# Routing in groups of 3, 3, 2 and 1 token tiles, with the mixes four tiles ahead

## The reference

```
mix = concatenate([y_ml, y_rg], axis=-1).astype(x.dtype) @ lp['w_out']
x = x + g1 * mix
hn2 = rmsnorm(x, lp['norm2']) * (1 + sc2) + sh2
...
s = jax.nn.sigmoid(x2d.astype(jnp.float32) @ router_w.astype(jnp.float32))
sb = s + router_bias.astype(jnp.float32)
grp = sb.reshape(N, N_GROUPS, N_EXPERTS // N_GROUPS)
gscore = jnp.sum(lax.top_k(grp, 2)[0], axis=-1)
_, gidx = lax.top_k(gscore, TOPK_GROUPS)
...
_, eidx = lax.top_k(jnp.where(emask, sb, -jnp.inf), TOP_K)
wts = wts / jnp.sum(wts, axis=-1, keepdims=True) * ROUTED_SCALE
```

## Time and profile before

| | us |
|---|---|
| median of 3 runs (2456.18 to 2460.27) | 2458.14 |
| the profiled execution | 2452.43 |
| its span, first to last instruction | 2450.7 |
| PE busy | 2045.1 (83%) |
| DVE busy | 1286.7 (53%) |
| ACT busy | 1012.7 (41%) |
| POOL busy | 689.4 (28%) |

### The profile page before, as it was taken

How to read it: one execution, slowest core, us unless ns; L and a number is a source line. 1 busy time by engine, 2 the same in 40 slices (tenths; PEclk the granted TensorE clock), 3 DMA queues, 4 the chain that set the end, 5 groups by cost and what they waited for, 6 DMA issues and landing times. The chain is left out here.

```text
span 2450.7 us, 30697 instructions
## 1 busy us (share of the span) xinstructions
PE 2045.1 (83%) x8155; PEld 1336.8 (55%) x8156; DVE 1286.7 (53%) x2145; ACT 1012.7 (41%) x1458; POOL 689.4 (28%) x648
## 2 busy tenths in 40 slices
PE   2776998999868979817999999999999999999940
PEld 0232433447767835405766666676666666666730
DVE  1547343300456758855555555565555454555547
ACT  0334433200112311105665555666665555556631
POOL 4010010000000012452344444443444444444420
PEclk7898998999879989958999999999999999999975
DMA  9422230110100063109978989867888989996454
GB/s 264 132 81 85 69 104 18 43 35 18 27 1 1 6 252 117 69 28 340 320 205 282 318 249 323 231 172 198 247 278 273 351 268 317 299 301 176 106 149 180
DMA packets 114241, 424.52 MB, mean 173 GB/s; under 512 B 22933, under 2 KB 37269, under 8 KB 89229
## 3 DMA queue, kind: packets, MB, share of 16 engines
q1 hardware_dynamic: 62508, 261.05, 28.8%
q0 software_dynamic: 51376, 162.80, 26.4%
q10 hardware_dynamic: 304, 0.02, 0.0%
HBM read 338.68 MB, written 85.66 MB: 173 GB/s over the span
## 5 line engine op out<-in xcount | busy, mean ns | idle before, releaser
L1726 DVE TENSOR_TENSOR wupl<-w,wuph 128x2048 fp32r<-128x2048 f32 x232 | 521.4, 2289 | 546.4 <-ACT wuph L1692 546.4
L1692 ACT ACTIVATE wuph<-w 128x2048 fp32r x232 | 432.0, 1916 | 37.9 <-SPq L1522 34.0
L1643 PE MATMUL bank<-w,hT 128*128 x912 | 414.1, 597 | 0.7 <-issue 0.3
L1625 PE MATMUL bank<-wuph,xTh 128*128 128x512 f32 x920 | 370.1, 402 | 22.1 <-DVE xTl L1735 22.0
L1625 PE MATMUL bank<-wuph,xTl 128*128 128x512 f32 x920 | 361.9, 393 | 0.0
L1625 PE MATMUL bank<-wupl,xTh 128*128 128x512 f32 x920 | 361.0, 392 | 0.0
L1643 PEld LDWEIGHTS bank<-w,hT 128*128 128x128 f32 x912 | 165.0, 191 | 169.2 <-issue 169.1
L1577 POOL DMA_INDIRECT xg<-hn_scratch,idx_g x118 | 215.4, 1825 | 96.0 <-POOL idx_g L1569 93.9
L1585 POOL DMA_INDIRECT yacc_scratch<-y,idx_s x114 | 185.1, 1623 | 113.8 <-ACT y L1683 67.0
L1682 ACT ACTIVATE y<-bank 128x512 f32<-128x512 f32 x114 | 68.2, 598 | 358.1 <-POOLq L1582 201.9
L1625 PEld LDWEIGHTS bank<-wuph,xTh 128*128 128x128 f32 x920 | 174.6, 190 | 61.3 <-issue 27.5
(11 more groups left out here) (312 smaller groups left out, 2340.9 us busy)
## 6 DMA issues: line engine op xcount, KB each, us to landing
w<-in_exp_w SPq DMA_DIRECT2D x192, 1024.0 KB, 9.0
wada<-in_w_ada POOLq DMA_DIRECT2D x16, 1024.0 KB, 5.9
wg<-in_w_in SPq DMA_DIRECT2D x12, 1024.0 KB, 5.5
x<-x_scratch SPq DMA_DIRECT2D x18, 512.0 KB, 4.0
wada<-in_w_ada SPq DMA_DIRECT2D x4, 2048.0 KB, 21.2
yacc_scratch<-zero POOLq DMA_DIRECT2D x10, 512.0 KB, 9.1
x_scratch<-x SPq DMA_DIRECT2D x9, 512.0 KB, 2.6
hn_scratch<-hn SPq DMA_DIRECT2D x9, 512.0 KB, 2.9
```

The source lines that it names most:

```text
L1625: mm = pe.matmul(b_up[j][:, :], x[:, k, :], w[:, :, k, :], start=(k == 0 and i == 0), stop=(k == KT - 1 and i == 2))
L1643: mm = pe.matmul(b_down[half][:, :], hT[:, i, :], w2[:, bass.ds(slot, 1), i, half * 512:(half + 1) * 512].rearrange("p s n -> p (s n)"), s ...
L1692: act.activation(part13(wup[j][0], half), raw13(e % WSLOT, half), ACT.Copy).then_inc(w_high, 1)
L1726: dve.tensor_tensor(part13(wup[j][1], half), raw13(e % WSLOT, half), part13(wup[j][0], half).bitcast(F32), ALU.subtract).then_inc(w_low, 1)
```

## The change

x and hn get six buffers each (NB = 6), and the mixes three pairs of banks in place of two. The tiles are handled in GROUPS of 3, 3, 2 and 1. For a group DVE takes all residuals, then works out one root for all its columns, then makes its rows one after the other. The first group's residuals, root and rows stand ahead of everything; a later group's residuals lie one by one between the choice and the slots of the tiles of the group before, and its root and rows behind the last of them. ACT squares the tiles of the next group behind the exponential (NEXT) and ahead of the ranks. PE runs mixes 0 to 3 at the start; mix t+4 comes in two halves, one between the transposes and the score of tile t, one between the score and the counts. SP loads six x tiles at the start and stores group by group.

The core of the diff:

```diff
+    NB = 6
+    GROUPS = [(0, 1, 2), (3, 4, 5), (6, 7), (8,)]
+    LEAD = 4
+    NEXT = {t: after[j] for group, after in zip(GROUPS, GROUPS[1:]) for j, t in enumerate(group) if j < len(after)}
...
-            for t in range(1, NT):
+            for t in range(1, NB):
                 load_x(t)
-                store(t - 1)
-            store(NT - 1)
+            for group in GROUPS:
+                for t in group:
+                    store_x(t)
+                for t in group:
+                    store_h(t)
+                    if t + NB < NT:
+                        load_x(t + NB)
...
+            def mix(t, half):
+                if t >= 3 and half == 0:
+                    pe.wait_ge(x2_new, t - 2)
...
-            mix(0)
+            for t in range(LEAD):
+                mix(t, 0)
+                mix(t, 1)
             pe.wait_ge(s_in, m.n_route)
             for t in range(NT):
-                if t + 1 < NT:
-                    mix(t + 1)
                 pe.wait_ge(hn_new, t + 1)
...
+                if t + LEAD < NT:
+                    mix(t + LEAD, 0)
                 bank = ring.fill()
...
                 ring.filled(mm)
+                if t + LEAD < NT:
+                    mix(t + LEAD, 1)
                 if t >= 1:
                     places(t - 1)
...
                 ring.drained(act.activation(ex[t % 2][:, :], bank[:, 0:NE], ACT.Exp, scale=-1.0))
+                if t in NEXT:
+                    square(NEXT[t])
                 if t >= 1:
                     place_out(t - 1)
...
+            def norm(group):
+                dve.wait_ge(x2_sq, group[-1] + 1)
+                c = slice(group[0], group[-1] + 1)
+                v = ss[:, c]
                 link(dve.tensor_scalar(v, v, 1.0 / D, EPS, ALU.mult, ALU.add))
-                newton_rsqrt(link, dve, v, rs[:, :], rt[:, :], ri[:, :])
...
+                newton_rsqrt(link, dve, v, rs[:, c], rt[:, c], ri[:, c])
+                for t in group:
+                    s, h = min(t, 1), hn[t % NB]
+                    link(dve.scalar_tensor_tensor(h[:, :], x[t % NB][:, :], rs[:, t:t + 1], scale[s], ALU.mult, ALU.mult))
+                    dve.tensor_tensor(h[:, :], h[:, :], shift[s], ALU.add).then_inc(hn_new, 1)
...
-            residual(0)
-            for t in range(NT):
-                if t + 1 < NT:
-                    residual(t + 1)
-                pick(t)
-                if t >= 1:
-                    slots(t - 1)
+            for t in GROUPS[0]:
+                add(t)
+            norm(GROUPS[0])
+            for group, after in zip(GROUPS, GROUPS[1:] + [()]):
+                for j, t in enumerate(group):
+                    pick(t)
+                    if j < len(after):
+                        add(after[j])
+                    if t >= 1:
+                        slots(t - 1)
+                    if j + 1 == len(after):
+                        norm(after)
```

More of the change, by code:

```diff
@@ L1138, in stage_route @@
         n2row = sb("n2row", [P, D])
-        x = [sb(f"x2_{j}", [P, D]) for j in range(2)]
-        hn = [sb(f"hn2_{j}", [P, D]) for j in range(2)]
+        x = [sb(f"x2_{j}", [P, D]) for j in range(NB)]
+        hn = [sb(f"hn2_{j}", [P, D]) for j in range(NB)]
         sq = sb("sq4", [P, D])
@@ L1178, in load_x, with store_x, store_h @@
             def load_x(t):
[L1179 to L1185, removed]
+                if t >= NB:
+                    sp.wait_ge(hn_new, t - NB + 1)
+                    sp.wait_ge(s_x2[0], 48)
+                sp.dma_start(x[t % NB][:, :], m.x1[t * P:(t + 1) * P, :]).then_inc(s_x[(t // 3) % 2], 16)
+            def store_x(t):
                 sp.wait_ge(x2_new, t + 1)
-                sp.dma_start(m.x2[rows, :], x[t % 2][:, :]).then_inc(s_x2[t % 2], 16)
+                sp.dma_start(m.x2[t * P:(t + 1) * P, :], x[t % NB][:, :]).then_inc(s_x2[t >= 3], 16)
+            def store_h(t):
                 sp.wait_ge(hn_new, t + 1)
-                sp.dma_start(m.hn2[rows, :], hn[t % 2][:, :]).then_inc(s_hn[t % 2], 16)
+                sp.dma_start(m.hn2[t * P:(t + 1) * P, :], hn[t % NB][:, :]).then_inc(s_hn[t >= 3], 16)
             load_x(0)
@@ L1228, in _ @@
             ring = Ring(pe, m.ring, full, free)
[L1230 to L1238, removed]
+            def mix(t, half):
+                if t >= 3 and half == 0:
+                    pe.wait_ge(x2_new, t - 2)
+                bank = m.banks[2 + 2 * (t % 3) + half]
+                for k in range(KT):
+                    mm = pe.matmul(bank[:, :], m.yT[:, k, t * P:(t + 1) * P], wo[:, k, half * 512:(half + 1) * 512],
+                                   start=(k == 0), stop=(k == KT - 1))
+                if half:
+                    mm.then_inc(mixed, 1)
             def places(t):
@@ L1257, in _ @@
                         kk = 4 * half + k
-                        mm = pe.transpose(bank[:, k * P:(k + 1) * P], hn[t % 2][:, kk * P:(kk + 1) * P], m.ident)
+                        mm = pe.transpose(bank[:, k * P:(k + 1) * P], hn[t % NB][:, kk * P:(kk + 1) * P], m.ident)
                     ring.filled(mm)
+                if t + LEAD < NT:
+                    mix(t + LEAD, 0)
                 bank = ring.fill()
@@ L1287, in place_out, with square @@
                 ring.drained(act.activation(rank[t % 2][:, :], bank[:, 0:NE], ACT.Copy))
-            for t in range(NT):
+            def square(t):
                 act.wait_ge(x2_new, t + 1)
@@ L1292, in _ @@
                     act.wait_ge(x2_sq, t)
-                act.activation(sq[:, :], x[t % 2][:, :], ACT.Square, accum_out=ss[:, t:t + 1]).then_inc(x2_sq, 1)
+                act.activation(sq[:, :], x[t % NB][:, :], ACT.Square, accum_out=ss[:, t:t + 1]).then_inc(x2_sq, 1)
+            for t in GROUPS[0]:
+                square(t)
+            for t in range(NT):
                 for half in range(2):
@@ L1320, in _, with add @@
                 link(dve.scalar_tensor_tensor(scale[s], scale[s], 1.0, n2row[:, :], ALU.add, ALU.mult))
-            def residual(t):
+            def add(t):
                 s = min(t, 1)
                 dve.wait_ge(mixed, t + 1)
[L1325 to L1329, removed]
+                dve.wait_ge(s_x[(t // 3) % 2], 48 * (t // NB + 1))
+                if t >= NB:
+                    dve.wait_ge(s_hn[0], 48)
+                    dve.wait_ge(full, jobs(t - NB) + 2)
+                h = hn[t % NB]
@@ L1330, in residual @@
                 for half in range(2):
                     c = slice(half * 512, (half + 1) * 512)
-                    ins = dve.tensor_tensor(h[:, c], m.banks[2 + 2 * (t % 2) + half][:, :], gate[s][:, c], ALU.mult)
+                    ins = dve.tensor_tensor(h[:, c], m.banks[2 + 2 * (t % 3) + half][:, :], gate[s][:, c], ALU.mult)
                 link(ins)
-                dve.tensor_tensor(x[t % 2][:, :], x[t % 2][:, :], h[:, :], ALU.add).then_inc(x2_new, 1)
-                dve.wait_ge(x2_sq, t + 1)
```

11 lines of the change are left out of this document (4 added, 7 removed).

## The result

The changed kernel takes 2500.29 us (median of 4 runs, 2493.22 to 2500.73), the kernel before 2457.56 in the same comparison: a ratio of 1.0164, 95% interval 1.0149 to 1.0178. It is slower by 42.7 us. A later comparison gave 2494.99 against 2451.27, 1.0177 (1.0161 to 1.0192).

What follows compares the result with a forecast made beforehand. DVE was taken to bound routing, PE 1.8 us a tile behind. Start, loop and clock put the end of tile 7's slots 41.9 us later: 2452.4 became 2494.3, plus 5.7 for timed runs, 2500.0 us; range 2483 to 2508.

Steps and rivals of the forecast that it cites:

- waits for counts: DVE's choice waits for PE's counts, which now stand behind half a mix: 1.6 us, four times.
- waits for ranks: DVE's slots wait for ACT's copy of the ranks, queued behind a square: 1.4 us, five times.
- tail of the stage: Count, last scatters and experts behind the slots of tile 7: unchanged.
- The start: Start of routing: DVE needs three mixes, PE runs four; first choice 26.9 us later, 941.9 in place of 915.05.
- The loop: Turns of tiles 1 to 4: a chain through all engines takes 20.7 us a tile, against 19.3 before.
- Rival (A): Added waits are covered in part; with both covered PE sets 16.6 us between choices: +22.9, 2481.0 us; chance 0.15.
- The clock: PE's clock falls after standstills: 1.7 us each at mixes 6 and 8, 3.1 at row 3, 6.5 in sum.
- The term of 1.7 for mixes 6 and 8: PE stands still some 4 us a tile in the loop; the slower clock then costs each mix 1.7 us.
- the term of 3.1 at row 3: PE stands still 14 us ahead of row 3's transposes; restarting its clock costs 3.1 us.
- Rival (C): Clock does not come back within a mix; mixes 6 to 8 run at the lower level: +76.8, 2534.9 us; chance 0.04.
- What goes: DVE's savings in routing: five roots, 15.6 us, and waits for squares, 12.2 us; together 27.8 us.
- Rival (B): DVE's 27.8 us saving comes through, with PE's order at the start costing nothing: 2430.3 us; chance 0.03.

Runs made afterwards that it cites:

- with PE kept busy: Changed kernel with unread products put where PE stands still (4 between transposes of tiles 2 and 4, 16 ahead of tile 3's): 2490.67 us, ratio 1.0141.
- the two runs with half of mixes 2 and 3: Mixes 2 and 3 use 4 of 8 products per half: stage 263.8 us in the changed kernel (273.5 without), 226.6 in the kernel before (229.4 without).
- the run with a root each: Changed kernel with the root worked out for each tile again, just ahead of its row: 2492.15 us against 2494.99; stage 277.1 against 273.7.
- the root behind the choice: Kernel before with root and row of tile t+1 moved behind the choice of tile t: 2448.29 us against 2450.65, ratio 0.9983.

## Why the prediction was right

It was 2500.0 us with a range of 2483 to 2508; measured were 2500.29. That the numbers are so close is in part luck: the profiled execution was put at 2494.3 and took 2500.73, that is 0.4 us above the median of its runs and not 5.7 below, as before. By the medians the change cost 42.7 us where 41.9 were forecast. The steps (all times from the stage's start):

| step | predicted | measured |
|---|---|---|
| first choice later by | 26.9 | 26.5 (67.8 - 41.3) |
| choice 0 to 1 | 16.6 | 16.4 |
| choice 1 to 2 | 20.7 + 1.7 clock | 23.7; 20.7 with PE kept busy |
| choice 2 to 3 | 31.2 + 3.1 clock | 32.7; 31.2 with PE kept busy |
| choice 3 to 4 | 20.7 + 1.7 clock | 23.0, of it 1.7 clock and 0.6 the late exponential; 20.8 with PE kept busy |
| choice 4 to the end of slots 7 | 72.6 | 73.1 |
| end of slots 7 later by | 41.9 | 42.1 (236.65 - 194.5) |
| waits for counts | 4 of 1.6 | 4, 5.9 in all |
| waits for ranks | 5 of 1.4 | 5, 6.6 in all |
| tail of the stage | unchanged | +1.9 |
| DVE busy in the stage | some 16 less | 12.2 less (157.03 - 144.87) |
| PE idle ahead of row 3, clock behind it | 14, near 0.5 | 14.65, 0.50 over the transposes |

**The start** held: DVE needs three mixes, PE runs four, and the two runs with half of mixes 2 and 3 show that this work is on the path in the changed kernel (7.0 us) more than before (2.8).

**The loop** held in its places and its length. Each of its two waits was taken out alone and both together, and what came back each time was more than the waits that DVE's list shows: the ranks' 6.6 us on DVE were worth 16.3 (18.9 with the small waits), since they held PE's transposes, too, and its clock fell at that stop. Rival (A), that the waits are covered, is out.

**The clock** was mis-sized in both directions. The term of 1.7 for mixes 6 and 8 was 3.0 and 1.7; the term of 3.1 at row 3 was 1.5. The sum, 6.5, came out at 6.2, and a late exponential added 0.6 that no term stood for. In the changed kernel's second profile the same three steps were 22.0, 33.5 and 24.4 us; without the exponential's 1.2 that is 1.3, 2.3 and 2.6 of clock loss, 6.2 in all. So one and the same stop cost 3.0 us in one execution and 1.3 in the other. That the sum is the same in both can be chance: in the run with half of mixes 2 and 3 these stops cost 8.3. Rival (C), a clock that stays low over whole mixes, is out: second halves were at 7.1 us throughout. The Trainium skill (TensorE: Matmul & The Clock Gate, "A second HAM failure mode: psum-queue depth-cycling") says that frequent short idle times between groups of matmuls make the clock swing between its levels and cost throughput. This case's trace agrees: the granted clock was 0.50 in the transposes behind the stops of 3.89 and 14.65 us and 1.00 in the second half mix of turn 2, and the stops cost 3.0 and 1.5 us.

**What goes** was taken as 27.8 us less on DVE, and the prediction said that the start alone uses it up. That was right, and the run with a root each sharpens it: of 15.6 us of roots at most 3.4 are real. The gain had been given to an engine that no longer bounds.

**Rival (B)**, faster, had its point at 939.0 us for the first choice plus all idle time after it. The start came at 941.6 on that clock (915.05 + 26.5), with 31 us of idle time ahead of choices 1 to 4 alone.

**Not foreseen** was the tail's +1.9 us, and the 1.1 and 2.8 us outside the stage; together with the 42.1 us of the steps they make the profile's span 47.9 longer, while the medians differ by 42.7.

**The range.** Its lower end has a slip: no clock loss at all is +35.4, and 2458.1 + 35.4 is 2493.5, not 2491. Nothing of the result hangs on it.

## What to carry to other kernels

When several engines pass one another work by queues in a fixed order, write down for a single turn what stands ahead of each hand-over on every engine: a wait that is put ahead of a small copy can close a loop through all of them, and then the turn costs the sum of its parts, not the largest. Saving work on the engine that bounds is worth nothing behind a start that makes it wait longer than the saving. In a profile, take small waits that have nothing to do with an edit off its gain before the gain is explained: here they were 2.6 us, once more than all that the edit gave. Where DVE waits only for a short answer of another engine, putting independent work in between, as with the root behind the choice, takes the wait without any of this.

## What the runs showed of the hardware

- PE's clock after a stop: standing for 2.2 to 14.7 us ahead of transposes was followed each time by a slower stretch (granted clock 0.50, the lower of its two levels, behind the stops of 3.89 and 14.65 us; eight transposes of 1.94 to 1.97 us instead of 1.04, half mixes of 7.5 to 9.6 instead of 7.03), and the loss did not grow with the stop: 3.0 us after 3.9, 1.5 after 14.65. The same stop of 3.9 us cost 3.0 us in one execution of the changed kernel and 1.3 in another. Products that nobody reads, put into the stops, kept the halves behind them at 7.03 and gave 6.1 us of stage.
- DVE lost some 2 us in a row of small dependent operations, 0.4 to 1.1 us at a time, with nothing that the profile shows to wait for, behind the slots of tile 7, in both profiled executions of the changed kernel, in its form with a root each and in one form of the kernel before, and not in the other nine profiles. The cause is open.
- A root of three columns on DVE took 3.2 and 3.4 us in the changed kernel (924.63 to 927.80, 999.66 to 1003.06), one of one column 3.1.
